# A three-layer block on one core: layer 2's attention takes its softmax sums and head outputs ahead of the convolution branch's steps, and the branch's roots go operation by operation

## The chip, the cores and the metric

One core of a Trainium2 chip runs the whole program in one launch. The time is the device time of one execution in microseconds (us). PE is the matmul engine (TensorE), DVE is VectorE, ACT is ScalarE, POOL is GpSimd, SP issues the DMAs. Every engine takes its own instructions strictly in the order in which the program lists them; engines wait for each other through semaphores.

## The reference

Three different layers run on 1024 tokens of 1024 features. The change is in the second, a hybrid layer. What matters of it:

```python
def hybrid_layer(h, cos, sin, chunk_id, ...):
    n = rms_norm(h, mix_norm_g)
    z = n @ w_in
    a, gate, c_q, c_kv, k_r = split(z)
    u = a * sigmoid(gate)                              # 512 features
    u = causal_depthwise_conv(u, conv_w, conv_b)       # 31 taps
    u = silu(layer_norm_2(u, conv_ln_g, conv_ln_b))    # over the 512 features
    q = rms_norm(c_q, q_norm_g) @ w_uq                 # 8 heads of 96
    kv = rms_norm(c_kv, kv_norm_g) @ w_ukv
    o = block_causal_attention(q, k, v, chunk_id)      # softmax(q k^T) v, chunks of 64
    mix = concatenate([rms_norm(u, conv_out_g), rms_norm(o, attn_out_g)])
    h = h + mix @ w_out
    ...                                                # then a feed-forward part
```

So the attention and the branch of `u` (convolution, layer norm, Silu, RMS norm) don't need each other before `mix`, and the kernel runs them side by side.

## The kernel before, in words

Data lie transposed: 128 features on the partitions, tokens along the free axis (1040 tokens here, in rows of 1044). `Mixer2` is layer 2's mixing part. Its attention has 8 heads. A head's keys go in three pieces of 4, 7 and 9 key tiles (`PIECES2`), so a head has 20 **slots** and the stage 160 (`CHUNKS2`); slot c is slot s of head h, with c = 20h + s. All three engines' programs (`pe` L1785, `act` L1960, `dve` L2185) are one loop over the slots, with the same things in the same slots:

- every slot: PE makes the scores of the chunk two slots on (`pe_chunk`), ACT takes their exponential (`act_exp`), and PE weighs the values with the chunk of this slot (`pe_weigh`).
- slots 0 to 5: the next head's keys (every second head) and queries on PE (`pe_next_head`, through one PSUM bank), copied by ACT and rotated by DVE (`act_products`, `dve_products`).
- slots 8 to 15: one block each of the next head's scores (`pe_score`), whose maxima DVE takes (`dve_max`). A score waits for the maximum two blocks back. In slots 15 and 18 PE turns the maxima into rows, which ACT copies.
- a piece ends in slots 3, 10 and 19. In the slot of the end ACT copies the weighed values and their sums (`act_head_copy`); the next piece's first `pe_weigh` waits for that copy. Two slots on PE turns the sums (`pe_column`) and DVE inverts them (`dve_inverse`); four slots on PE spreads the inverses (`pe_spread`) and DVE multiplies (`dve_head_out`). So DVE inverts in slots 5, 12 and 1 and writes head outputs in slots 7, 14 and 3.
- PE's chunks, rows, columns and spreads, and the branch's sums, take the same three PSUM banks in turn (`pe_ring` L1627): each waits until the one three before it has been copied or used.

Beside this runs the **branch**, written as a generator for each engine (`pe_branch` L1462, `act_branch` L1483, `dve_branch` L1515). `taps(c)` says how many of its steps slot c takes: `STEPS` of them are spread evenly over the first `LAST_STEP` = 140 slots, after 61 that run ahead of the attention. DVE's branch is 124 convolution taps, three adds, then per 128 features (4 of them) the centring and the adding of squares, the root of the variance (`root_newton` L409, four operations in a row), the scaling, again the adding of squares, a second root, and the last scaling. ACT's branch is the copies of the sums, the squares, the first guess of the root (Ln, then Exp), the four Silus in one step, four more squares and a second guess. PE's branch is three groups of three matmuls against ones. A `yield` ends a step, and bare `yield`s are the delays that hold the three engines' branches together:

```python
    def taps(self, c):
        done = [min(x, self.LAST_STEP) * self.STEPS // self.LAST_STEP for x in (c, c + 1)]
        return done[1] - done[0]
```

In the loops, `advance(branch, self.taps(c))` stands ahead of `pe_column` and `pe_spread` on PE, of `act_head_copy` on ACT, and of `dve_inverse` and `dve_head_out` on DVE.

Of the kernel before, what the change touches and what calls it, by code (L numbers as in the profile page):

```python
# [7 lines left out]
P = 128  # L8
# [8 lines left out]
LN_EPS, EPS = 1e-5, 1e-6  # L17
# [126 lines left out]
def advance(steps, n):  # L144

    for _ in range(n):
        if next(steps, None) is None:
            return
# [19 lines left out]
class Core:  # L168
# [240 lines left out]
    def root_newton(self, v, out, scratch, sums, n, eps, inc=None, sums_taken=None):  # L409
        v.tt(scratch, out, out, ALU.mult)  # L410
        v.settle()
        v.stt(scratch, sums, n * eps, scratch, ALU.add, ALU.mult, inc=sums_taken)
        v.settle()
        v.ts(scratch, scratch, -0.5 / n, 1.5, ALU.mult, ALU.add)
        v.settle()
        v.tt(out, out, scratch, ALU.mult, inc=inc)
        v.settle()

    def ones_of(self, view, pieces, banks):
# [961 lines left out]
class Mixer2:  # L1381
# [13 lines left out]
    SMALL = (0, 4, 8)  # L1395
    STEPS, LAST_STEP = 91, 140

# [64 lines left out]
    def pe_branch(self, t):  # L1462

        k = self.k
        for _ in range(CONV2 * 4 + 2):
            yield True
        for n, summed in enumerate((1, 8, 13)):
            t.wait_ge(self.u_step_v, summed)
            self.u_ring.append([])
            for t0, m in THREE:  # L1470
                r, bank = self.pe_ring(t)
                t.mm([(k.ps[:, bank, 0:m], k.ones[:, :], self.A[0][:, t0:t0 + m], True, True)], self.filled)
                self.u_ring[n].append(r)
            yield True
            for _ in range((5, 12, 0)[n]):
                yield True
# [6 lines left out]
    def act_branch(self, a):  # L1483
        k, A, M = self.k, self.A, self.M
# [8 lines left out]
        for n in range(2):  # L1493
# [5 lines left out]
            yield True  # L1499
            yield True  # L1500
            if n:
# [4 lines left out]
            for c in range(4):  # L1506
                a.act(M[c], M[c], ACT.Silu, scale=k.column("conv_ln_g_2", c), bias=k.column("conv_ln_b_2", c), inc=self.u_step_a)
            yield True
            a.settle()
# [5 lines left out]
    def dve_branch(self, v):  # L1515
# [23 lines left out]
        for n in range(2):  # L1539
# [3 lines left out]
            v.wait_ge(self.u_step_a, (5, 14)[n])  # L1543
            v.settle()
            k.root_newton(v, A[1], A[2], A[3], 4 * P, EPS, inc=self.u_step_v)
            yield True
            if n:
                break
            for c in range(4):
                v.tt(M[c], M[c], A[1], ALU.mult, inc=self.u_step_v if c == 3 else None)  # L1550
                yield True
            yield True
            for c in range(4):
# [231 lines left out]
    def pe(self, t):  # L1785
# [28 lines left out]
        for c in range(len(CHUNKS2)):  # L1814
# [9 lines left out]
            if h + 1 < H2 and s in self.ROW_AT:  # L1824
                for p in self.ROW_AT[s]:
                    self.pe_row(t, h + 1, p)
            advance(branch, self.taps(c))
            if self.ended(c - 2) is not None:
                self.pe_column(t, self.ended(c - 2))
            if self.ended(c - 4) is not None:  # L1830
                self.pe_spread(t, self.ended(c - 4))
            self.pe_weigh(t, c)
            k.label(("slot", c))
# [126 lines left out]
    def act(self, a):  # L1960
# [24 lines left out]
        for c in range(len(CHUNKS2)):  # L1985
# [6 lines left out]
            if h + 1 < H2 and s in self.ROW_AT:  # L1992
                for p in self.ROW_AT[s]:
                    self.act_row(a, h + 1, p)
            advance(branch, self.taps(c))
            if self.ended(c) is not None:
                self.act_head_copy(a, c)
            if c >= self.LAST_STEP + 4 and c % 4 == 0:
                self.act_u_row(a, (c - self.LAST_STEP) // 4 - 1)
# [185 lines left out]
    def dve(self, v):  # L2185
# [30 lines left out]
        for c in range(len(CHUNKS2)):  # L2216
            h, s = divmod(c, A_HEAD)
            self.dve_products(v, ("fill", c))
            if h + 1 < H2 and s in self.SCORE_AT:
                self.dve_max(v, item)  # L2220
                item += 1
            advance(branch, self.taps(c))
            if self.ended(c - 2) is not None:
                self.dve_inverse(v, self.ended(c - 2))
            if self.ended(c - 4) is not None:
                self.dve_head_out(v, self.ended(c - 4))
            if c >= self.LAST_STEP + 4 and c % 4 == 0:
                self.dve_u_row(v, (c - self.LAST_STEP) // 4 - 1)
# [1137 lines left out]
```

## Time and profile before

| | us |
|---|---|
| runs shown: median of 3 (lowest, highest) | 3708.06 (3707.95, 3716.88) |
| the profiled execution: its time | 3714.25 |
| its span (first to last instruction) | 3712.1 |
| PE busy in the span | 3475.0 |
| layer 2's attention, roughly | 1509 to 1830 of the span |

How to read it: PE is the engine that the whole kernel waits for in most places, so what PE loses in the attention is lost to the kernel. In the timeline rows, the number in brackets is the time for which the engine stood idle just before the instruction, and behind the arrow what ended that idle time. PEclk is the mean of the granted TensorE clock over a window, 1.00 being 2.4 GHz and 0.50 being 1.2 GHz. A busy time of PE includes what a lower clock adds. Lines are those of the kernel; helpers such as L96 (`tt`), L105 (`stt`), L124 (`act`), L129 (`copy`) and L136 (`mm`) carry most operations.

### The profile page before, as it was taken

To read this page: it belongs to the slowest core of one execution; us is meant where nothing else is said; L and a number is where in the kernel's file an instruction comes from. 1 tells how busy PE (TensorE), PEld (TensorE's weight loads), DVE (VectorE), ACT (ScalarE), POOL (GpSimd) and SP (SyncE) were. 2 spreads that over 40 slices of the span, in tenths; PEclk is the share of its full clock that TensorE was granted. 3 is DMA by queue.
4 is the path that set the end of the run, shared out by engine and by line. 5 is a ranking of instruction groups with operands and counts; after the bars stand their busy time and mean duration, and the time that the engine had idled before them with its cause. 6 is when DMAs were issued, how large, how long until landed. Compare 5 with 4: busy or idle time off the path is not lost.

```text
span 3712.1 us, 39245 instructions
## 1 busy us (share of the span) xinstructions
PE 3475.0 (94%) x16240; PEld 2806.7 (76%) x16240; DVE 1769.8 (48%) x1897; ACT 1119.0 (30%) x1492; POOL 1069.5 (29%) x1144
## 2 busy tenths in 40 slices
PE   9988999999999999898899999999998999999997
PEld 6655667888887688555588998998976777777776
DVE  4567562222223678686455544644664222443422
ACT  4333352111112522444531111111234222322332
POOL 3111343223323233000023433433432222211243
PEclk9999999999999999999899999999999999999999
DMA  3000211111111211000111111111121111100232
GB/s 121 23 24 28 103 62 63 51 47 46 49 48 58 75 63 40 12 6 6 58 40 40 46 46 51 41 49 49 46 91 35 68 57 40 35 24 28 85 122 93
DMA packets 56249, 192.21 MB, mean 52 GB/s; under 512 B 6900, under 2 KB 7284, under 8 KB 55560
## 3 DMA queue, kind: packets, MB, share of 16 engines
q1 hardware_dynamic: 56072, 189.71, 14.9%
q8 instruction: 128, 2.10, 0.2%
q14 instruction: 49, 0.40, 0.0%
HBM read 172.83 MB, written 16.86 MB: 51 GB/s over the span
## 4 chain that ended last, share of the span: by engine, by line
PE 78%; DVE 14%; ACT 5%; issue 2%; DMA 1%; POOL 0%; DVEq 0%; ACTq 0%; SPq 0%; POOLq 0%
PE psum L263 21%; PE psum L264 21%; PE psum L265 21%; PE psum L136 11%; DVE mix L105 3%; DVE work L96 3%; PE psum L305 2%; PE psum L307 1%; PE psum L306 1%; DVE res L96 1%; ACT L124 1%; DVE res L105 1%; DVE softmax_shift_columns L111 1%; DVE u_padded L96 1%; DVE work L114 1%
## 5 line engine op out<-in xcount | busy, mean ns | idle before, releaser
L96 POOL TENSOR_TENSOR w_lo<-w_raw,w_hi 128x256 fp32r<-128x256 f32 x1140 | 1069.3, 969 | 2607.7 <-ACT w_hi L129 2607.7
L263 PE MATMUL psum<-x_hi,w_hi 128*128 128x512 f32 (+2 forms) x3264 | 1229.6, 377 | 36.0 <-issue 6.8
L264 PE MATMUL psum<-x_lo,w_hi 128*128 128x512 f32 (+2 forms) x3264 | 1183.8, 363 | 0.0
L265 PE MATMUL psum<-x_hi,w_lo 128*128 128x512 f32 (+2 forms) x3264 | 1180.6, 362 | 0.0
L129 ACT CAST w_hi<-w_raw 128x1024 fp32r<-128x1024 f32 x285 | 298.2, 1048 | 1619.1 <-PE psum L265 1524.6
L263 PEld LDWEIGHTS psum<-x_hi,w_hi 128*128 128x128 f32 x3264 | 621.5, 190 | 141.5 <-issue 37.6
L264 PEld LDWEIGHTS psum<-x_lo,w_hi 128*128 128x128 f32 x3264 | 622.2, 191 | 91.0 <-issue 19.8
L265 PEld LDWEIGHTS psum<-x_hi,w_lo 128*128 128x128 f32 x3264 | 620.3, 190 | 78.7
L263 PE MATMUL psum<-h_hi,w_hi 128*128 128x512 f32 x848 | 338.3, 399 | 15.5 <-issue 9.0
L265 PE MATMUL psum<-h_hi,w_lo 128*128 128x512 f32 x848 | 336.0, 396 | 0.0
L264 PE MATMUL psum<-h_lo,w_hi 128*128 128x512 f32 x848 | 333.8, 394 | 0.0
L105 DVE SCALAR_TENSOR_TENSOR res<-res,psum 128x1024 f32<-128x1024 f32 (+1 forms) x88 | 90.3, 1027 | 253.6 <-PE psum L265 245.4
L263 PEld LDWEIGHTS psum<-h_hi,w_hi 128*128 128x128 f32 x848 | 160.0, 189 | 56.8 <-issue 13.2
L264 PEld LDWEIGHTS psum<-h_lo,w_hi 128*128 128x128 f32 x848 | 160.0, 189 | 40.0 <-issue 2.6
L265 PEld LDWEIGHTS psum<-h_hi,w_lo 128*128 128x128 f32 x848 | 159.9, 189 | 35.7
L136 PE MATMUL psum<-res 128*65 128x256 f32 (+5 forms) x480 | 171.5, 442 | 7.9 <-ACT res L129 4.2
L96 DVE TENSOR_TENSOR h_tmp<-h_tmp 128x1024 f32<-128x1024 f32 (+1 forms) x36 | 54.8, 1523 | 248.2 <-ACT h_tmp L124 248.2
L105 DVE SCALAR_TENSOR_TENSOR mix<-u_padded,vectors,mix 128x1044 f32<-128x1044 f32 x120 | 168.5, 1404 | 5.0 <-ACT work L129 0.8
L96 DVE TENSOR_TENSOR up<-psum,ffn_rms 128x1026 f32<-128x1026 f32 x44 | 54.0, 1227 | 204.7 <-PE psum L265 204.7
L105 DVE SCALAR_TENSOR_TENSOR up_conv<-up,vectors,up_conv 128x1024 f32<-128x1024 f32 x88 | 143.9, 1635 | 3.1
L305 PE MATMUL psum<-x_hi,w_hi 128*128 128x348 f32 (+2 forms) x304 | 122.7, 403 | 20.5 <-DVE x_lo L96 11.5
L96 DVE TENSOR_TENSOR res<-res,psum 128x1024 f32<-128x1024 f32 (+1 forms) x56 | 68.5, 1224 | 151.5 <-PE psum L265 148.5
(281 smaller groups left out, 3671.5 us busy)
## 6 DMA issues: line engine op xcount, KB each, us to landing
w_raw<-w_dram SPq DMA_DIRECT2D x285, 512.0 KB, 3.2
res<-spill SPq DMA_DIRECT2D x4, 1044.0 KB, 9.6
res<-x_dram SPq DMA_DIRECT2D x8, 512.0 KB, 7.7
res<-x_dram SPq DMA_DIRECT2D x4, 1024.0 KB, 8.2
spill<-res SPq DMA_DIRECT2D x1, 4096.0 KB, 13.9
spill_a<-mix SPq DMA_DIRECT2D x8, 512.0 KB, 2.6
res<-spill_a SPq DMA_DIRECT2D x8, 512.0 KB, 4.3
x_plain<-spill SPq DMA_DIRECT2D x4, 1024.0 KB, 10.9
```

The source lines that it names most:

```text
L96: self.mark(self.e.tensor_tensor(out, a, b, op), inc)
L105: self.mark(self.e.scalar_tensor_tensor(out, a, s, b, op0, op1), inc)
L111: self.mark(self.e.tensor_reduce(out, a, AX.X, op, negate=negate), inc)
L114: self.mark(self.e.reciprocal(out, a), inc)
L124: self.mark(self.e.activation(out, a, func, bias=bias, scale=scale), inc)
L129: self.mark(self.e.copy(out, a), inc)
L136: ins = self.e.matmul(out, lhsT, rhs, start=start, stop=stop, skip_group_check=True)
L263: t.e.matmul(out, whi, xhi, start=k == 0, stop=False, skip_group_check=True)
L264: t.e.matmul(out, whi, xlo, start=False, stop=False, skip_group_check=True)
L265: ins = t.e.matmul(out, wlo, xhi, start=False, stop=last_k, skip_group_check=True)
L305: t.e.matmul(out, whi, xhi, start=first, stop=False, skip_group_check=True)
L306: t.e.matmul(out, whi, xlo, start=False, stop=False, skip_group_check=True)
```

## The change

Four edits. In the slot loops of all three engines the branch's steps move behind the inverses and head outputs (DVE), the head copy (ACT), and the columns and spreads (PE). DVE's root becomes four steps instead of one (`root_steps`, new). The Silus go in two steps of two. The number of steps over the 140 slots goes from 91 to 98, and the delays on PE and ACT grow to match, so every step of the branch gets a new slot.

```diff
--- before.py
+++ after.py
@@ -415,6 +415,22 @@
         v.settle()
         v.tt(out, out, scratch, ALU.mult, inc=inc)
         v.settle()
+
+    def root_steps(self, v, out, scratch, sums, n, eps, inc=None):
+
+        v.settle()
+        v.tt(scratch, out, out, ALU.mult)
+        yield True
+        v.settle()
+        v.stt(scratch, sums, n * eps, scratch, ALU.add, ALU.mult)
+        yield True
+        v.settle()
+        v.ts(scratch, scratch, -0.5 / n, 1.5, ALU.mult, ALU.add)
+        yield True
+        v.settle()
+        v.tt(out, out, scratch, ALU.mult, inc=inc)
+        v.settle()
+        yield True
 
     def ones_of(self, view, pieces, banks):
         return [(self.ps[:, b, 0:m], self.ones[:, :], view[:, t0:t0 + m], True, True) for b, (t0, m) in zip(banks, pieces)]
@@ -1393,7 +1409,7 @@
     SCORE_AT = {8: 3, 9: 8, 10: 2, 11: 7, 12: 1, 13: 6, 14: 4, 15: 5}
     ROW_AT = {15: (0,), 18: (1, 2)}
     SMALL = (0, 4, 8)
-    STEPS, LAST_STEP = 91, 140
+    STEPS, LAST_STEP = 98, 140
 
     def __init__(self, core, ffn):
         self.k, self.ffn, s = core, ffn, core.s
@@ -1472,7 +1488,7 @@
                 t.mm([(k.ps[:, bank, 0:m], k.ones[:, :], self.A[0][:, t0:t0 + m], True, True)], self.filled)
                 self.u_ring[n].append(r)
             yield True
-            for _ in range((5, 12, 0)[n]):
+            for _ in range((5, 16, 3)[n]):
                 yield True
 
     def act_sums(self, a, n, out, scale):
@@ -1497,7 +1513,8 @@
             a.settle()
             k.root_guess(a, A[1], A[3], 4 * P, EPS, self.u_step_a)
             yield True
-            yield True
+            for _ in range(4):
+                yield True
             if n:
                 break
             for _ in range(4):
@@ -1505,7 +1522,8 @@
             a.wait_ge(self.u_step_v, 10)
             for c in range(4):
                 a.act(M[c], M[c], ACT.Silu, scale=k.column("conv_ln_g_2", c), bias=k.column("conv_ln_b_2", c), inc=self.u_step_a)
-            yield True
+                if c % 2:
+                    yield True
             a.settle()
             for c in range(4):
                 a.wait_ge(self.u_step_v, (10, 10, 11, 12)[c])
@@ -1541,14 +1559,13 @@
             yield True
             yield True
             v.wait_ge(self.u_step_a, (5, 14)[n])
-            v.settle()
-            k.root_newton(v, A[1], A[2], A[3], 4 * P, EPS, inc=self.u_step_v)
-            yield True
+            yield from k.root_steps(v, A[1], A[2], A[3], 4 * P, EPS, inc=self.u_step_v)
             if n:
                 break
             for c in range(4):
                 v.tt(M[c], M[c], A[1], ALU.mult, inc=self.u_step_v if c == 3 else None)
                 yield True
+            yield True
             yield True
             for c in range(4):
                 if c:
@@ -1824,11 +1841,11 @@
             if h + 1 < H2 and s in self.ROW_AT:
                 for p in self.ROW_AT[s]:
                     self.pe_row(t, h + 1, p)
-            advance(branch, self.taps(c))
             if self.ended(c - 2) is not None:
                 self.pe_column(t, self.ended(c - 2))
             if self.ended(c - 4) is not None:
                 self.pe_spread(t, self.ended(c - 4))
+            advance(branch, self.taps(c))
             self.pe_weigh(t, c)
             k.label(("slot", c))
         self.pe_column(t, 3 * H2 - 1)
@@ -1992,9 +2009,9 @@
             if h + 1 < H2 and s in self.ROW_AT:
                 for p in self.ROW_AT[s]:
                     self.act_row(a, h + 1, p)
-            advance(branch, self.taps(c))
             if self.ended(c) is not None:
                 self.act_head_copy(a, c)
+            advance(branch, self.taps(c))
             if c >= self.LAST_STEP + 4 and c % 4 == 0:
                 self.act_u_row(a, (c - self.LAST_STEP) // 4 - 1)
             k.cast(a, k.at["slot", c][0])
@@ -2219,11 +2236,11 @@
             if h + 1 < H2 and s in self.SCORE_AT:
                 self.dve_max(v, item)
                 item += 1
-            advance(branch, self.taps(c))
             if self.ended(c - 2) is not None:
                 self.dve_inverse(v, self.ended(c - 2))
             if self.ended(c - 4) is not None:
                 self.dve_head_out(v, self.ended(c - 4))
+            advance(branch, self.taps(c))
             if c >= self.LAST_STEP + 4 and c % 4 == 0:
                 self.dve_u_row(v, (c - self.LAST_STEP) // 4 - 1)
         self.dve_inverse(v, 3 * H2 - 1)
```

## Rows read from the trace of the kernel before

**Rows 1.** The page: busy time of each engine; the chain that ended last.

```profile
PE 3475.0 (94%) x16240; PEld 2806.7 (76%) x16240; DVE 1769.8 (48%) x1897; ACT 1119.0 (30%) x1492; POOL 1069.5 (29%) x1144
...
PE 78%; DVE 14%; ACT 5%; issue 2%; DMA 1%; POOL 0%; DVEq 0%; ACTq 0%; SPq 0%; POOLq 0%
```

**Rows 2.** Windows per head (3 to 6): us, busy of PE, PEld, DVE, ACT, POOL; PEclk.

```profile
1622.00:1660.00 38.00, 35.88 (x160) 23.16 (x159) 28.54 (x43) 16.84 (x46) 0.00 (x0) 0.91 0.01 1
1660.00:1697.00 37.00, 33.30 (x158) 20.03 (x156) 31.77 (x51) 14.36 (x44) 5.89 (x4) 1.00 0.04 15
1697.00:1748.00 51.00, 39.05 (x173) 24.16 (x172) 31.33 (x46) 27.85 (x61) 0.00 (x0) 0.93 0.00 0
1748.00:1800.00 52.00, 39.99 (x156) 23.00 (x157) 26.31 (x45) 30.47 (x56) 2.77 (x4) 0.83 0.03 11
```

**Rows 3.** Timeline of heads 4 and 5: start, length, engine, what, [idle before <-releaser].

```profile
1682.96 1.16 DVE L111 TENSOR_REDUCE softmax_shift_columns<-psum 128x1 fp32r<-128x960 f32 x1 [0.91 <-PE psum L136]
...
1695.39 0.70 PE L136 MATMUL psum<-work,x_plain 97*128 97x256 f32 x2 [1.56 <-DVE mix L96]
...
1702.78 0.43 PE L305 MATMUL psum<-x_hi,w_hi 128*128 128x348 f32 x1 [0.49 <-ACT x_hi L124]
...
1703.85 1.92 PE L136 MATMUL psum<-u_padded,ones 128*128 128x348 f32 x6
```

**Rows 4.** Groups of instructions from 1500 to 1835 us: busy, mean ns | idle before.

```profile
L105 DVE SCALAR_TENSOR_TENSOR mix<-u_padded,vectors,mix 128x1044 f32<-128x1044 f32 x61 | 82.0, 1345 | 2.9 <-ACT work L129 0.8
...
L96 DVE TENSOR_TENSOR u_padded<-u_padded 128x1044 f32<-128x1044 f32 x12 | 15.0, 1247 | 21.8 <-ACT u_padded L124 21.5
...
L124 ACT ACTIVATE u_padded<-mix 128x1044 f32<-128x1044 f32 x11 | 11.8, 1073 | 6.7 <-DVE mix L96 4.8 <-DVE u_padded L96 1.8
...
L124 ACT ACT_TABLE_LOAD x7 | 9.0, 1283 | 0.1
...
L124 ACT ACTIVATE mix<-mix,vectors 128x1044 f32<-128x1044 f32 x4 | 4.7, 1246 | 0.0
...
L124 ACT ACTIVATE u_padded<-u_padded,tiny 128x1044 f32<-128x1044 f32 x2 | 2.3, 1168 | 0.0
```

**Rows 5.** Timeline of heads 5 and 6: PE's waits, and one operation of a root.

```profile
1716.52 0.86 PE L136 MATMUL psum<-res 16*65 16x384 f32 x2 [1.08 <-ACT res L129]
...
1729.57 0.70 PE L136 MATMUL psum<-work,x_plain 97*128 97x256 f32 x2 [3.17 <-DVE mix L96]
...
1730.60 3.21 PE L136 MATMUL psum<-u_padded,ones 128*128 128x348 f32 x6
...
1742.08 0.70 PE L136 MATMUL psum<-work,x_plain 97*128 97x256 f32 x2 [1.77 <-ACT res L124]
...
1744.35 0.70 DVE L102 TENSOR_SCALAR u_padded<-u_padded 128x1044 f32<-128x1044 f32 x1
...
1747.89 1.22 PE L136 MATMUL psum<-work,x_plain 97*128 97x256 f32 x2 [4.17 <-DVE mix L96]
...
1756.95 0.43 PE L305 MATMUL psum<-x_hi,w_hi 128*128 128x348 f32 x1
...
1766.97 0.91 PE L136 MATMUL psum<-work,x_plain 97*128 97x384 f32 x2 [3.44 <-ACT res L124]
...
1770.11 1.54 PE L136 MATMUL psum<-res 16*65 16x384 f32 x2 [2.23 <-ACT res L129]
...
1783.09 0.70 PE L136 MATMUL psum<-work,x_plain 97*128 97x256 f32 x2 [0.41 <-DVE mix L96]
...
1793.80 0.70 PE L136 MATMUL psum<-work,x_plain 97*128 97x256 f32 x2 [1.77 <-ACT res L124]
...
1799.61 1.22 PE L136 MATMUL psum<-work,x_plain 97*128 97x256 f32 x2 [4.17 <-DVE mix L96]
```

**Rows 6.** Windows: slots 9 to 16 of head 1, and of head 6.

```profile
1573.00:1586.00 13.00, 12.10 (x51) 8.38 (x50) 12.29 (x25) 3.58 (x10) 0.00 (x0) 0.74 0.00 1
...
1782.00:1800.00 18.00, 11.65 (x57) 7.73 (x55) 13.38 (x25) 9.02 (x16) 0.00 (x0) 0.89 0.00 1
```

## The prediction

> **What bounds the kernel now.** Three views, in this order. The page: PE is busy for 94% of the span and holds 78% of the chain that ended last [rows 1], so a time won elsewhere counts only where PE waits for it. Windows over the attention, one per head, each from slot 16 of the head before to its own slot 15: head 3 takes 38 us and head 4 37 us, with the convolution's taps beside them, but heads 5 and 6, beside which the norms, roots and Silus run, take 51 and 52 us [rows 2]. That is 28 us more, of which PE's work is about 6 (the branch's matmuls against ones, one group of three 1.92) [rows 3]. The timeline says where the rest sits. In head 4 PE waits 1.56 us at slot 16 for the head output that DVE writes in slot 14 [rows 3]. In heads 5 and 6 it waits 1.08 us for a head copy that ACT makes after a square, 3.17 us for a head output behind DVE's additions, 1.77 us twice for an exponential behind Ln and Exp, 4.17 us twice for a head output behind the four operations of a root, and 3.44 and 2.23 us for ACT behind the Silus [rows 5]. The granted clock comes on top: 0.93 and 0.83 in these heads against 1.00 in head 4 [rows 2]. At two levels, 0.5 and 1, this is 7.1 and 17.7 us at 1.2 GHz, and the drops stand behind the waits: after the 2.23 us wait two matmuls take 1.54 us.
>
> **The new places.** With 98 steps over 140 slots, a slot takes 0.70 steps in place of 0.65, 14 per head in place of 13. Counting yields gives the slots. The taps end at slot 89 (was 96). First sums: 94 (was 101). Squares on ACT and centrings on DVE: 95, 97, 98, 99 (were 103, 104, 106, 107). Second sums 102 (110), Ln and Exp 104 (112), root on DVE 105, 107, 108, 109 (all in 113). Scaling 111, 112, 114, 115 (115 to 119). Silus 117 and 118 (all in 121). Second squares 119, 121, 122, 124 (123 to 127). Third sums 127 (130), Ln and Exp 128 (132), root 129, 131, 132, 134 (133). Last scalings end in slot 139 as before. What matters is the kind of slot: slots 0 to 5 of a head hold the next head's queries, about 3 us of PE each, slots 15 to 19 hold about 1 us of PE each. I work out PE's time part by part.
>
> **A. Heads 0 to 3: 0 us** (bounds -2 and +4). DVE is nearly full between slots 9 and 16: 12.3 of 13 us [rows 6]. From the start of the big maximum at 1682.96 to the head output are 12.4 us with four taps of 1.35 in them [rows 3, 4]. Afterwards three taps lie there (slots 9, 11, 12), since slot 13 has none and slot 14's stands behind the head output: -1.3. But the steps of slots 7 and 8 now lie ahead of the maximum with the head output of slot 7 in front: about +0.9. In heads 1 and 3 PE also runs at the lower level there (0.74) and is as late as DVE [rows 6], so these win nothing: 2 x -0.45. Against it, behind the head output DVE has five taps instead of four before the next rotation of queries, for which PE waits in two of the heads: about +1.
>
> **B. Slots 94 to 101: +8.3 us** (0 to +11). The three adds (3 x 1.25 [rows 4]) take the place of one tap in head 4, head output +0.65 later. The third group of ones needs the bank that this head output frees, so PE stands in slot 14 and not in 16, with about 2.6 us of work still ahead. Then the chain of squares: DVE centres (1.25), ACT squares (1.07), DVE adds (1.25), three times over: about 3.65 us a round [rows 4]. It used to lie beside queries; now it lies in slots 95 to 99, where PE needs about 5 us for all five. ACT takes its queue in order. Behind square 1 wait the exponential of slot 98 and the rows; behind square 2 the exponential of slot 99 and the head copy that slot 100 needs; behind square 3 the copy of the first keys, which frees the bank of the second. Laid out from the head output, with these lengths, square 1 ends at 7.7 us, square 2 at 11.3, square 3 at 14.8, and the second piece of keys starts at 17.0. Before, from the wait's end to that piece are 7.4 us [rows 3]. Of the 9.6 more, 1.92 are the first sums, which used to come right after it: +7.7, and with the 0.65 +8.3.
>
> **C. Head 5: -8.4 us** (-11.5 to -5). The four waits of 1.08, 3.17, 1.77 and 4.17 go [rows 5]: the head copy and head output stand in front of the step, the root is in four slices of at most 1.25, and Ln and Exp (two loads of 1.28, 1.17 and 1.07: 4.8 us of ACT [rows 4]) lie in a slot with queries. In their place: about 1.7 us in slot 106 or 107, where PE has 4.0 us of work against ACT's 5.75, and about 1.4 at slot 16, where DVE's chain is 10.8 us (12.4 less four taps, plus a slice and two scalings of 1.25). -10.2 + 3.1 = -7.1. The group of ones that took 3.21 us at 1.2 GHz takes 1.92: -1.3 [rows 3, 5].
>
> **D. The Silus: +2.0 us** (-5.7 to +9). The old waits of 3.44 and 2.23 go: -5.7 [rows 5]. But Silu and Exp alternate: slot 118's exponential lies between the two pairs, and each change of function has a load of 1.28 us in front [rows 4], four instead of two: +2.6 us of ACT. From slot 16's head output on: ACT ends its exponential at 1.7, loads, waits for the last scaling (3.9), does two Silus of 1.25 (6.4), loads, the exponential (8.2), rows, load, two Silus (12.6), load, exponential, head copy (14.8), square, copy of the queries (16.8). PE reaches the second piece of queries at 16.8 us; before it took 1756.95 - 1747.89 = 9.06 [rows 5]: +7.7.
>
> Of such loads the rule of the Trainium skill, ScalarE: Activation LUTs, section Rules for kernel authors, speaks against this split: do all functions of one table set before switching. The same page (What ACT_TABLE_LOAD costs) gives about 2.66 us a switch, load and drain; the row shows 1.28 and under 0.1 us of idle around it. By the page's figure the two extra switches would be an estimated 5.3 us instead of 2.6, and the sum of all parts about -0.2 us instead of -2.9.
>
> **E. Head 6: -3.9 us** (-6.4 to 0). Old waits: 1.77 + 4.17 and 0.41 behind a head output, 6.35 in all [rows 5]. Ln and Exp start four slots earlier, in slot 8; Exp ends some 5.2 us after slot 8's start, and behind it DVE has three slices (1.25, 1.25, 0.70) and 5.6 us of reductions and head output (12.4 less the taps and the first maximum), so slot 14's head output is done after 14.0 us, against 11.6 us of PE work [rows 5, 6]: about 2.4 remain.
>
> **F. The clock: -0.9 us** (-7 to +5). Old: 24.8 us at 1.2 GHz in heads 5 and 6, worth at most half. 1.3 of it is in C, 1.9 in D's 9.06; of the rest I take 6.9 as on PE's path. New knots of waits in B and D (each 5 to 9 us of waiting within 17) should bring drops as before, 3.4 to 6.8 us each, more after D: +6.0.
>
> **At nothing:** PE's columns and spreads, which moved only past matmuls of the branch; SP and POOL, which issue and do nothing for it (the branch has no DMA); the four slices of a root, which are the same four operations. If their cover goes, it is PE's wait for a spread, at most one operation of 1.25 us.
>
> **Sum:** 0 + 8.3 - 8.4 + 2.0 - 3.9 - 0.9 = **-2.9 us**. The profiled execution took 3714.25, so 3711.3 by its own time; it lies 6.2 us above the median of the runs shown, 3708.06. Carried to the median: **3705**. A measurement of this kernel tells about 0.3%, 11 us, from no change.
>
> **The rivals.**
> - **The waits go and none comes (24%).** If DVE and ACT run far enough ahead that B's chain ends under PE's next work, B is near 0 and D is two waits of 2 us. For it: chunks are made two slots ahead, and heads 3 and 4 cost 37 to 38 us. Against it: ACT's own idle time is small in slots with Silus. Of the 22 us of excess that isn't work, two thirds go: -15, so 3693.
> - **ACT's queue in short slots becomes the wait (18%), slower.** Place: slots 95 to 101 and 117 to 120. Its price is all three rounds of squares (3 x 3.65 = 11) and the full D at +4, with +4 of clock; C and E then give back only 5 and 2, as ACT starts them late. 11 + 4 + 4 - 5 - 2 = +12: 3720. It decides from the point at which PE passes slots 95 to 99 in 5 us and the copies of slots 99 and 100 stand behind squares 2 and 3. For it: the 1.08 us wait is this very thing in a longer slot.
> - **Nothing moves (15%).** Waits only change their names, as slots 9 to 16 are bound by DVE's reductions with or without a step among them: within 2 us, 3708.
> - **Forecast (43%):** gains and losses of 8 us cancel, 3705.
>
> The clock has a rival inside the forecast: if the knots in B and D bring no drop, F is -6.9 and the result is 3699. The Trainium skill, TensorE: Matmul & The Clock Gate, Terms, puts the penalty at the throttled time times (1 - K/N), here half. By that the old 24.8 us are worth 12.4 at most; rows agree on the factor, since matmuls there take twice as long, but PE was not always the bound.
>
> Range: 3690 (the first rival, a little past it) to 3720 (the second). Faster by over 0.3%: the first rival, 0.24. Slower: the second, 0.18. Same: 0.58.
>
> **What would show it.** Heads 0 to 4 unchanged within 1 us each. The four 1.77 and 4.17 waits gone, none over 2 us behind a head output in heads 5 and 6. PE waits for ACT at slots 98 to 101 of some 7 us in all, and at slots 118 to 121 of 8 to 10 us, with drops of the clock behind both. Nine table loads instead of seven. I am wrong in B if the second keys of head 5 start less than 12 us after the head output of head 4, in D if PE waits less than 5 us around the Silus, in A if the first four heads differ by over 4 us together.

## The result, and the profile after

The kernel before took 3712.12 us (median of 17 runs, 3707.06 to 3716.88), the changed one 3718.05 (17 runs, 3710.17 to 3726.10). The ratio is 1.0015, 95% interval 1.0009 to 1.0021: **5.6 us slower**, where 2.9 us faster was forecast. The 17 runs put the median of before 4 us above the three runs of the prediction. The profiled execution of the changed kernel took 3710.17, the shortest of its 17, so its span must not be compared as a whole; stage by stage it can.

The page has the same instructions as before, two more on ACT (the table loads), and 3.3 us more of PE [rows 1].

```profile
PE 3478.3 (94%) x16240; PEld 2810.0 (76%) x16240; DVE 1769.4 (48%) x1897; ACT 1121.9 (30%) x1494; POOL 1068.5 (29%) x1144
...
PE 78%; DVE 14%; ACT 5%; issue 2%; DMA 1%; POOL 0%; DVEq 0%; ACTq 0%; SPq 0%; POOLq 0%
```

Layer 2's attention, from its first row of maxima on PE to the first L263 matmul behind the last head, as one window. Columns: length; busy of PE, PEld, DVE, ACT, POOL; PEclk; DMA share; GB/s. Two profiles of the kernel before, the second taken later:

```profile
1509.03:1829.97 320.94, 280.30 (x1219) 168.89 (x1219) 216.85 (x334) 151.71 (x377) 19.82 (x16) 0.93 0.02 7
```

```profile
1512.62:1835.15 322.53, 281.85 (x1218) 169.71 (x1219) 216.82 (x334) 151.84 (x377) 19.83 (x16) 0.92 0.02 7
```

And three of the changed kernel:

```profile
1506.13:1833.54 327.41, 294.65 (x1219) 180.63 (x1219) 216.16 (x334) 154.51 (x379) 20.83 (x16) 0.89 0.02 7
```

```profile
1509.60:1837.42 327.82, 295.11 (x1218) 180.73 (x1218) 216.08 (x334) 154.50 (x379) 20.83 (x16) 0.89 0.02 7
```

```profile
1510.27:1837.66 327.39, 294.66 (x1219) 180.62 (x1219) 216.07 (x334) 154.50 (x379) 20.83 (x16) 0.89 0.02 7
```

The stage repeats within 1.6 us and is 5.8 us longer (327.5 against 321.7), which is the whole difference of the medians. Length less busy time is PE's idle time: 40.6 and 40.7 us before, 32.8, 32.7 and 32.7 after. So **the change took 7.9 us of waiting away from PE**. But the same 1219 matmuls are 13.7 us longer (294.8 against 281.1), and PEclk fell from 0.93 to 0.89. The granted clock has two levels here, 2.4 and 1.2 GHz, and the time at 1.2 GHz in the stage is 48 and 51 us before and 75 us in each of the three profiles after; half of the 25 us more is 12.6.

What costs is the part of that time in which PE has work. Before, PE was busy for 38.2 and 41.4 us of its time at 1.2 GHz, since waits lay in it; after, for 71.5, 72.2 and 71.6. Busy time less half of this, that is, PE's work at full clock, is 261.2 and 261.1 us before and 258.9 to 259.0 after. So the 5.8 us are 7.9 less of waiting, 2.3 less of work at full clock and 16.0 more for matmuls at 1.2 GHz. Both kernels have a stretch at 1.2 GHz near the end of head 6. In the kernel before it holds most of the 4.17 us wait that ends at 1799.61 [rows 5]; in the changed one it is full of work (8 matmuls, then 21):

```profile
1795.93:1802.75 6.82, 3.14 (x8) 1.96 (x8) 6.56 (x12) 0.76 (x4) 0.00 (x0) 0.50 0.00 0
```

```profile
1795.95:1802.77 6.82, 6.82 (x21) 5.30 (x22) 5.55 (x13) 1.15 (x3) 0.00 (x0) 0.50 0.00 0
```

By heads, each from the end of the head output of slot 14 (DVE) to that of the next head, for heads 5, 6 and 7; this is nearly the cut of [rows 2]:

```profile
1696.90:1751.81 54.91, 47.76 (x189) 29.51 (x188) 28.50 (x46) 29.33 (x66) 0.00 (x0) 0.84 0.00 0
1751.81:1804.28 52.47, 43.23 (x152) 26.72 (x153) 22.55 (x41) 32.58 (x57) 3.78 (x4) 0.77 0.03 10
1804.28:1828.51 24.23, 23.73 (x109) 12.61 (x107) 13.20 (x19) 13.04 (x37) 0.00 (x0) 1.00 0.00 1
```

Cut so, the first from the stage's start, heads 0 to 7 took 35.84, 39.62, 35.38, 39.61, 35.86, 52.49, 51.73, 25.38 us before and 35.30, 39.69, 37.81, 40.02, 37.95, 54.91, 52.47, 24.23 after. Head 7 took 26.9 us in the second profile of before, from a longer stretch at 1.2 GHz, and 24.2 to 24.3 in all three after, which have none there.

PE's waits in the timeline of heads 4 to 6 (start, length, what, idle before and who ended it):

```profile
1668.26 0.43 PE L305 MATMUL psum<-x_hi,w_hi 128*128 128x348 f32 x1 [1.62 <-DVE work L96]
...
1694.19 0.79 PE L136 MATMUL psum<-x_hi 96*128 96x512 f32 x1 [3.01 <-DVE softmax_shift_columns L96]
...
1695.42 3.69 PE L136 MATMUL psum<-u_padded,ones 128*128 128x348 f32 x6
...
1705.06 0.50 PE L136 MATMUL psum<-identity_rounded,softmax_shift_columns 128*1 128x128 f32 x5 [1.16 <-ACT res L124]
...
1715.16 0.66 PE L305 MATMUL psum<-x_hi,w_hi 128*128 128x348 f32 x1 [3.20 <-ACT x_hi L124]
...
1736.32 0.70 PE L136 MATMUL psum<-work,x_plain 97*128 97x256 f32 x2 [0.34 <-ACT res L124]
...
1751.86 0.70 PE L136 MATMUL psum<-work,x_plain 97*128 97x256 f32 x2 [0.29 <-DVE mix L96]
...
1759.87 1.65 PE L136 MATMUL psum<-work,x_plain 97*128 97x384 f32 x2 [4.41 <-ACT res L124]
...
1766.45 0.88 PE L136 MATMUL psum<-res 16*65 16x400 f32 x2 [1.07 <-ACT res L129]
...
1768.21 0.43 PE L305 MATMUL psum<-x_hi,w_hi 128*128 128x348 f32 x1 [0.46 <-ACT work L129]
...
1795.32 0.61 PE L136 MATMUL psum<-res 16*65 16x256 f32 x2 [2.02 <-ACT res L129]
```

What to see: the waits of 1.08, 3.17, 1.77, 4.17, 3.44 and 2.23 us [rows 5] are gone. New are 3.01 (a score in slot 14 of head 4), 3.20 (the second keys) and 4.41 (behind the Silus). And the first group of ones, 1.92 us before [rows 3], takes 3.69. ACT around the Silus:

```profile
1753.59 1.28 ACT L124 ACT_TABLE_LOAD   x1
1755.61 2.40 ACT L124 ACTIVATE mix<-mix,vectors 128x1044 f32<-128x1044 f32 x2 [0.73 <-DVE mix L96]
1758.03 1.28 ACT L124 ACT_TABLE_LOAD   x1
1759.32 0.49 ACT L124 ACTIVATE res<-psum 16x400 f32<-16x400 f32 x1
...
1760.59 1.28 ACT L124 ACT_TABLE_LOAD   x1
1761.89 2.40 ACT L124 ACTIVATE mix<-mix,vectors 128x1044 f32<-128x1044 f32 x2
1764.31 1.28 ACT L124 ACT_TABLE_LOAD   x1
1765.60 0.54 ACT L124 ACTIVATE res<-psum 64x64 f32<-64x64 f32 x2
```

It is the chain that the prediction laid out: load, two Silus, load, the exponential for which PE stands 4.41 us, and the same again.

### The profile page after: what moved, and what is told of

Read it like the earlier page. It is cut to its first block, busy times and chain, and to the rows that moved or that the text cites. A ratio compares the mean times of both kernels' runs of the same rounds, so it can differ in the third digit from the quotient of the medians.

```text
span 3708.1 us, 39248 instructions
## 1 busy us (share of the span) xinstructions
PE 3478.3 (94%) x16240; PEld 2810.0 (76%) x16240; DVE 1769.4 (48%) x1897; ACT 1121.9 (30%) x1494; POOL 1068.5 (29%) x1144
## 4 chain that ended last, share of the span: by engine, by line
PE 78%; DVE 14%; ACT 5%; issue 2%; DMA 1%; POOL 0%; DVEq 0%; ACTq 0%; SPq 0%; POOLq 0%
PE psum L263 21%; PE psum L265 20%; PE psum L264 20%; PE psum L136 11%; DVE mix L105 3%; DVE work L96 3%; PE psum L305 2%; PE psum L307 1%; PE psum L306 1%; DVE res L96 1%; ACT L124 1%; DVE res L105 1%; DVE softmax_shift_columns L111 1%; DVE work L114 1%; ACT res L124 1%
## 5 line engine op out<-in xcount | busy, mean ns | idle before, releaser
L263 PE MATMUL psum<-x_hi,w_hi 128*128 128x512 f32 (+2 forms) x3264 | 1227.6, 376 | 36.1 <-issue 6.8
L263 PEld LDWEIGHTS psum<-x_hi,w_hi 128*128 128x128 f32 x3264 | 620.5, 190 | 140.9 <-issue 37.2
L263 PE MATMUL psum<-h_hi,w_hi 128*128 128x512 f32 x848 | 337.7, 398 | 15.5 <-issue 9.0
L263 PEld LDWEIGHTS psum<-h_hi,w_hi 128*128 128x128 f32 x848 | 159.6, 188 | 56.7 <-issue 13.2
L96 DVE TENSOR_TENSOR h_tmp<-h_tmp 128x1024 f32<-128x1024 f32 (+1 forms) x36 | 55.1, 1531 | 249.3 <-ACT h_tmp L124 249.3
```

Source lines behind the costliest of these rows:

```text
L96: self.mark(self.e.tensor_tensor(out, a, b, op), inc)
L263: t.e.matmul(out, whi, xhi, start=k == 0, stop=False, skip_group_check=True)
```

## The experiments

Three theories stand in the expectations. **W**: waits and work alone count. **C**: what costs is the time that PE spends at 1.2 GHz. **O**: the new order costs by itself. "Stage" is the window above; "at 1.2 GHz" is its time there; "run at 1.2 GHz" is the mean over all timed runs (of before, 121) of 2 x (1 - granted clock) x time. Each ratio is against runs of before timed together with that kernel. A "long" slot is one of slots 0 to 5 of a head, which hold the next head's queries; a "knot" is a place where several waits follow each other; the "rhythm" is which slots get the branch's steps.

| kernel | median us (runs) | ratio to before [95%] | stage | PE busy | PE idle | at 1.2 GHz | run at 1.2 GHz |
|---|---|---|---|---|---|---|---|
| before | 3712.1 (17) | | 320.9, 322.5 | 280, 282 | 40.7 | 48, 51 | 227 |
| after | 3718.1 (17) | 1.0015 [1.0009, 1.0021] | 327.4 to 327.8 | 295 | 32.7 | 75 | 255 |
| order alone | 3719.8 (9) | 1.0023 [1.0013, 1.0032] | 326.6 | 288 | 38.1 | 62 | 244 |
| slices alone | 3716.0 (11) | 1.0010 [1.0001, 1.0019] | 324.9 | 284 | 41.2 | 45 | 221 |
| old places | 3712.8 (11) | 1.0007 [0.9997, 1.0017] | 320.8 | 288 | 32.7 | 55 | 239 |
| squares long | 3712.1 (11) | 1.0006 [0.9997, 1.0015] | 321.7 | 288 | 33.8 | 61 | 244 |
| Silus long | 3716.2 (11) | 1.0014 [1.0004, 1.0023] | 320.6 | 290 | 30.3 | 65 | 256 |
| both long | 3707.6 (11) | 0.9990 [0.9982, 0.9999] | 318.0 | 287 | 31.4 | 55 | 231 |

**Order alone.** The kernel before with only the moved calls, for example on ACT:

```diff
-            advance(branch, self.taps(c))
             if self.ended(c) is not None:
                 self.act_head_copy(a, c)
+            advance(branch, self.taps(c))
```

> The kernel before with only the order in the slots changed (sums, head copy and head output ahead of the branch's steps; 91 steps, root and Silus as before). Theory W (time in the stage follows PE's waits): the waits of 1.08 and 3.17 us in head 5 and 0.41 in head 6 go, the 4.17 and 1.77 us and the Silus' waits stay: 4 to 5 us of waits less, about 5 us faster than before. Theory C (what the change costs is PE's time at 1.2 GHz, which new places of waits bring): few waits move, so PE's time at 1.2 GHz from 1509 to 1834 us stays near the 49 us of before (73 in the change), and again 4 to 5 us faster. Theory O (the order itself delays DVE ahead of the big maximum, +0.9 us a head, and so costs in all heads): 0 to 4 us slower.

3719.8 us, so the new order in itself loses as much as the whole change. W and C both said 4 to 5 us faster and missed; O had the direction but neither the size (0 to 4) nor the places, since heads 0, 1, 3 and 4 are only 0.1 to 0.2 us longer and heads 2, 5 and 6 2.3, 1.1 and 0.9. Its idle time fell by 2.6 us; the 3.17 us wait became one of 3.63 and one of the two 4.17 us waits stayed. The time at 1.2 GHz did not stay near 49 us as C had it but rose to 62. In head 2 the 6.8 us at 1.2 GHz that in the kernel before end with head 1, in slots where PE waits for DVE, begin 6.8 us later, at the start of head 2, and fall on the chunks behind the head output, where PE has work.

**Slices alone.** The changed kernel with the three calls of `advance` back in their old places.

> The changed kernel with the attention's sums and values behind the convolution's steps again, as before the change: 98 slices, Silus two and two. If the order costs something of its own (theory O): the run is nearer to before, 3712, and head 2, which the order alone made 2.3 us longer, is 35.4 us again. If only the place of the 1.2 GHz stretches decides (theory C): the time goes with their sum in the stage by half of it, whatever that is: 320.9 - 8 + half of (sum - 48) us for the stage, within 2. If waits alone decide (theory W): the 1.77 and 3.17 us waits that the order removes come back, +3 to +5 over after: 3721 to 3723.

3716.0 us. The clock is as good as before (45 us), but idle time is 41.2 us: nothing of the 7.9 is won. By theory C I had taken the 8 us as given without the order, which makes a stage of 311; it was 324.9. W (3721 to 3723) missed too, and O only in part: head 2 came down to 36.35 us, not to 35.4, and the run is 4 us above before and 2 below after. The order and the slices take the waits away only together: -2.6 and +0.5 apart, -7.9 as one.

**Order and slices in the old places.** A table of slots in place of `STEPS`, 91 steps' rhythm, Silus together in slot 121:

```diff
-        done = [min(x, self.LAST_STEP) * self.STEPS // self.LAST_STEP for x in (c, c + 1)]
-        return done[1] - done[0]
+        return self.PLACES.count(c)
```

> The change with its order and its slices, but every step of the branch in the slot it had before (squares 103 to 107, root from 113 on, all Silus in 121, where queries are computed). Theory W: PE's waits of heads 5 and 6 are only those of the Silus (5.7 us) and of the two Ln and Exp (3.5), 12 us less than before: 10 to 14 us faster than before. Theory C: the same waits, and PE's time at 1.2 GHz falls below the 49 us of before: 12 to 16 faster. If the order and slices themselves cost (rival), it is within 3 us of before.

3712.8 us, stage 320.8. Its idle time is 32.7 us, that of the changed kernel to a tenth, yet the stage is 6.7 us shorter with 20 us less at 1.2 GHz. The waits that the change takes away go without its new rhythm; what the changed kernel loses against this one comes with the rhythm. But W and C, with 10 to 16 us of gain over before, both missed: the run is within 3 us of before, as the rival had it. The 7.9 us less of waiting are met by 7.0 us more of PE's busy time. That is again the clock: PE is busy for 53.1 us at 1.2 GHz against 38.2 and 41.4 before, though the stretches are only 5 us longer, and its work at full clock is 261.5 us against 261. Stretches that used to cover waits now cover work.

**One knot at a time into long slots.** The same table, with the squares in slots 100 to 103 and what follows them to 109; or with both Silu steps in slot 120 and the second squares in 121 to 124.

> The change with one block moved: the four squares and centrings go from slots 95 to 99 to slots 100 to 103, the second sums, Ln and Exp and root follow (104 to 109); all else as in the change. Theory W: the waits of 1.16, 0.62 and 3.20 us behind the squares go, about 4 us less, 1 to 3 us of new ones in slots 103 to 107: 2 to 4 us faster than the change, so 2 to 4 slower than before. Theory C: the 1.2 GHz stretches of 3.4 and 10.2 us that began at 1708 and 1715 go too, another 3 to 5 us: as fast as before or up to 3 us faster. Rival (queries' slots are no better): as slow as the change.

> The change with one block moved: both pairs of Silus go from slots 117 and 118 to slot 120, one behind the other, the squares follow in 121 to 124. Two table loads fewer (2.6 us of ACT). Theory W: PE's waits of 4.41, 1.07 and 0.46 us become one or two of together 4 to 6 us, as slot 120 has queries but the block is 7.5 us long: 0 to 2 us faster than the change. Theory C: the stretches of 1.2 GHz (6.8 and 3.4 us) stay, since the wait stays: the same 0 to 2. Rival (the two pairs' split is what costs): 5 or more us faster than the change.

3712.1 and 3716.2 us; stage 5.8 and 6.9 us shorter than after's, with the idle time changed by +1.1 and -2.4. Most of the gain is again PE's busy time, 6.9 and 4.5 us less. The squares came out as C had it, as fast as before. For the Silus the run fits W and C (0 to 2 us), the stage their rival (5 or more). Of their gain little reached the runs: their time at 1.2 GHz is 256 us, after's, though the stage has 10 less. What lies outside the stage must have had more; one profile doesn't show why.

> The changed kernel with the squares in slots 100 to 103, what follows them to slot 109, and both Silu steps in slot 120 with the squares behind them in 121 to 124: both knots that the change made are in long slots. If the two parts' gains add in the stage (after 327.4, squares alone 321.7, Silus alone 320.6): 315 us and 3706 for the run. If the 1.2 GHz stretches only move on (theory C): stage 318 to 326 us, with more than 60 us at 1.2 GHz in it, and the run 3712 to 3716.

3707.6 us, 10.4 us below after and faster than the kernel before by more than its interval. The stage fell by 9.5 us, its time at 1.2 GHz by 20 and its idle time by 1.4. The gains did not add to 315, as theory C had it, but the time at 1.2 GHz went lower than it allowed, and the run is shorter than its 3712 to 3716. By heads: the squares alone take 2.1 us off head 5 and 3.8 off head 6, the Silus alone 7.5 off head 6, both 2.1 and 7.6. So what the squares win in head 6 isn't won again beside the Silus.

```profile
1511.42:1829.46 318.04, 286.68 (x1218) 175.93 (x1219) 216.11 (x334) 151.88 (x377) 20.84 (x16) 0.91 0.02 7
```

**Work of no use in PE's idle time.** These kernels leave nothing out; they add matmuls whose product nobody reads, ahead of the slot's chunk:

```diff
+    def pe_idle_work(self, t, h, s):
+        if h < 6 and s in (10, 11, 12, 13, 14, 15, 16):
+            t.e.matmul(self.k.ps[:, 7, 0:512], self.ident_r[:, :], self.k.x_hi[:, 0, 0:512], start=True, stop=True, ...)
...
+            self.pe_idle_work(t, h, s)
             if c + 2 < len(CHUNKS2):
                 self.pe_chunk(t, c + 2)
```

| kernel | matmuls | median us (runs) | ratio to before [95%] | stage | PE idle | at 1.2 GHz |
|---|---|---|---|---|---|---|
| before, heads 0 to 5 | 42 | 3716.4 (11) | 1.0010 [1.0001, 1.0019] | 322.7 | 38.4 | 34 |
| before, heads 0 to 3 | 28 | 3715.8 (12) | 1.0008 [0.9999, 1.0017] | 322.0 | 39.2 | 41 |
| after, heads 0 to 5 | 42 | 3713.2 (11) | 1.0000 [0.9991, 1.0009] | 324.0 | 31.9 | 48 |
| after, heads 4 and 5 | 14 | 3719.8 (9) | 1.0027 [1.0017, 1.0036] | 327.0, 328.0 | 31.0, 30.4 | 75, 75 |
| after, heads 0 to 3 | 28 | 3710.7 (11) | 0.9992 [0.9983, 1.0001] | 323.9 | 30.2 | 58 |
| both long, heads 0 to 5 | 42 | 3705.5 (11) | 0.9986 [0.9978, 0.9995] | 317.9 | 30.1 | 34 |
| both long, heads 0 to 3 | 28 | 3705.9 (12) | 0.9982 [0.9974, 0.9990] | 317.6 | 32.0 | 37 |

> The kernel before with one more 128x512 matmul in each of slots 10 to 16 of heads 0 to 5 (42 in all, each about 0.27 us at 1.9 GHz), ahead of the slot's chunk: TensorE idles there for VectorE in heads 0 to 3. Its product is read by nobody. Theory C (what costs is the time that TensorE spends at 1.2 GHz, which follows its idle stretches): the time at 1.2 GHz in the stage falls from 47.9 us to 30 or less and the time by up to 9 us: 3702 to 3708 against 3712 median of before. Theory W (only waits and work count; the clock is chance that an edit of this kind does not steer): no difference in heads 0 to 3 and, in heads 4 and 5, whose slots have no idle time, 14 x 0.27 = +4 us: 3716. If the clock is unmoved and the slots are full: up to +11 us.

> The kernel after with the same 42 extra matmuls. Theory C: the time at 1.2 GHz in the stage falls from 74.6 us to 45 or less, and the run gets 5 to 12 us shorter than after: 3706 to 3712, the loss of the change gone. Theory W: +4 us or more over after's 3718: 3722. The difference between the changed and the unchanged kernel, both filled, is by theory C about -8 (the waits that the change takes away) and by theory W the same as without the fillers, +6.

(The 0.27 us are an estimate that no row shows by itself; the clock's levels here are 1.2 and 2.4 GHz.)

The same addition did opposite things. Before got 4 us longer: W's number, but not by W's way, since heads 4 and 5 are 0.4 us longer together and the stage is as long as in the second profile of before. After got 5 us shorter, 1 us above C's range. Filled, the changed kernel is 3 us faster than the unchanged one, where C had said 8 faster and W 6 slower. In the kernel before, the 6.8 us at 1.2 GHz at the ends of heads 1 and 3 vanished and these heads stayed at 39.6 us: those stretches lay where PE waited for DVE and had cost nothing. In the changed kernel head 5 fell from 54.9 to 51.7 us.

> The changed kernel with the extra matmuls in heads 4 and 5 alone (14 instead of 42). Where in heads 0 to 3 the clock drops in slots that wait for VectorE anyway, it should cost nothing there: then these 14 give the whole gain of the 42, run 3713 and head 5 at 51.7 us against 54.9 of after. If the drops of heads 0 to 3 cost too, or carry over into head 5, the gain is smaller: 3715 to 3718, head 5 at 53 us or more.

> The changed kernel with the extra matmuls in heads 0 to 3 alone (28). They took the stretches at 26 and 105 us away when all 42 were there, and the heads stayed as long as they were. If early stretches cost nothing and carry nothing over: 3718, as after, with head 5 at 54.9 us. If they carry over (a later stretch goes or moves because an earlier one went): head 5 or what is behind the stage gets shorter, run 3712 to 3715.

The first missed both its forecasts (3713, and 3715 to 3718): 3719.8. The second is the telling one. None of the 28 matmuls is in head 5, heads 0 to 4 are as long as in the changed kernel, and head 5 is 3.3 us shorter. Head 5 of the kernel with them (compare the first of the three rows by heads above):

```profile
1699.75:1751.37 51.62, 44.26 (x189) 27.31 (x188) 28.48 (x46) 29.14 (x66) 0.00 (x0) 0.89 0.00 0
```

The same 189 matmuls, 3.5 us less of PE. Where the time at 1.2 GHz went is seen one head earlier. Head 4 in the changed kernel, then with the 28 matmuls:

```profile
1658.95:1696.90 37.95, 32.02 (x140) 19.43 (x141) 32.90 (x49) 12.81 (x38) 5.89 (x4) 0.96 0.05 14
```

```profile
1661.82:1699.75 37.93, 34.70 (x140) 21.18 (x141) 32.89 (x48) 12.81 (x38) 5.89 (x4) 0.88 0.05 14
```

Head 4 has 6.1 us more at 1.2 GHz (9.5 against 3.4) and is as long as before, as PE waits less there (3.2 us against 5.9); head 5 has 6.1 us less (11.0 against 17.1). The two heads together have what they had, 20.5 us: the stretches moved from work onto a wait.

The run is 7 us shorter than after's, more than its stage gave (3.7); the rest is outside. What the matmuls did where they are, the same 7 us of head 0 (about its slots 10 to 14), in the changed kernel and then with them:

```profile
1532.13:1539.13 7.00, 7.00 (x24) 4.94 (x22) 6.64 (x13) 0.77 (x2) 0.00 (x0) 0.57 0.00 0
```

```profile
1535.16:1542.16 7.00, 6.94 (x34) 4.87 (x35) 6.64 (x13) 1.15 (x3) 0.00 (x0) 1.00 0.00 0
```

The clock stayed at 2.4 GHz instead of falling to 1.2, and 34 matmuls took the time of 24. DVE, for which PE waits here, had 13 operations in either. The 14 matmuls of heads 4 and 5 alone won nothing: the first profile had a shorter head 5 (51.5 us) but longer heads 3 and 4, from stretches at 1.2 GHz that came ahead of any added matmul. Was that the program or the draw?

> The kernel with 14 extra matmuls, profiled again. If the stretches are set by the program: at 122 and 163 us again, heads 3 and 4 at 41.6 and 39.3 us. If they are a draw of that execution: heads 3 and 4 as in the changed kernel, 40.0 and 37.9, head 5 at 51.5, and the stage 324.

> The changed kernel, profiled a third time. If set by the program: the same stretches as in the two profiles before it, stage 327 to 328 us, about 75 us at 1.2 GHz. If a draw: another stage length, between 313 and 325.

> The kernel before, profiled again. If the stretches at 1.2 GHz follow the program, they fall at the same places of the stage (69, 144, 223, 236, 260 and 288 us behind its start) within a few us and sum to 45 to 51 us; if they are chance, they fall elsewhere and the sum is anywhere from 35 to 75.

> The kernel after, profiled again. If the stretches at 1.2 GHz follow the program: at 28, 69, 86, 107, 148, 189, 202, 209, 253, 264, 274 and 291 us behind the stage's start and 70 to 80 us in sum, the stage 327 us. If they are chance: other places, a sum of 45 to 80, and a stage of 313 to 330 us that goes with half the sum; the waits of TensorE (3.01, 3.20, 4.41 us) are the same in either case.

All three profiles of the changed kernel have their stretches within 1 us of the same places, and the two of before theirs (the last 3.4 us longer in the second). The kernel with 14 had them in the changed kernel's places the second time, with a head 5 of 55.1 us. So in this stage the program sets them nearly always, and the first profile was an exception; what makes one is open. Outside the stage they do vary: the whole of the three profiles of the changed kernel holds 233, 264 and 257 us at 1.2 GHz, 158 to 188 of it outside the stage, and their times are 3710.2, 3717.5 and 3717.7 us.

> The kernel before with the extra matmuls in heads 0 to 3 alone. Its stretches at 68 and 143 us lie in slots that wait for VectorE, and with all 42 matmuls they were gone and nothing shorter. If the matmuls undo a loss that the change brought: 3712 to 3714, no gain, and the changed kernel with them (3710.7) is 1 to 4 us faster than this one. If they are a gain for any kernel of this kind: 3705 to 3708.

> The changed kernel with both knots in long slots and the extra matmuls in heads 0 to 3 alone. If their effects add (both long: 10 us off after; these matmuls: 7 off after): 3700 to 3703. If the stretches only find other places: 3705 to 3708, as with both long alone or with all 42.

Before: 3715.8, no gain, and 5 us slower than the changed kernel with the same 28 matmuls. So they undo a loss that the change brought. With both knots in long slots they give 3705.9, as all 42 do (3705.5): the stretches only find other places, and the effects don't add. For the 42 theory C had said 20 us less at 1.2 GHz, a stage 3 us shorter and 3703 to 3709: the first and last came, but the stage stayed (317.9 against 318.0), as PE's busy time went up by 1.1 us. The two kernels with both knots in long slots and added matmuls are the fastest of the study, 0.14 and 0.18% below the kernel before, 12 us below the changed one.

## Why the prediction was wrong

**The step that failed is F, the clock.** Forecast: old drops worth 6.9 us given back, "new knots" charged 6.0, so -0.9. Measured: 25 us more at 1.2 GHz in the stage and PE's busy time 13.7 us longer; the clock cost about +12 us (see the sum). Three things in the step were wrong. Its sizes: it took drops of 3.4 to 6.8 us for a knot, but around B's waits three stretches have 20.4 us at 1.2 GHz, and head 6, behind the Silus, went from 17.6 to 23.9. Its places: all three profiles have new stretches also at 27, 85 and 105 us behind the stage's start, in heads 0 and 2, for which the prediction had put zero. Where they lie, only the one at 85 us costs (3.4 us long, on keys and queries), since heads 0 and 2 are as long without the other two, which the 28 matmuls took away. In head 0 no wait is new; in head 2 the one for the queries' rotation grew from 0.47 to 1.63 us, as forecast in A, and the 1.57 us one for the head output went. And it treated the clock as the waits' shadow, which should lighten when waits go. In the whole-stage rows, less waiting and more time at 1.2 GHz stand together, and a stretch that held a wait before holds work after.

The factor was right. PE's busy time in the stage, less half of its busy time at 1.2 GHz, is 261 us in both profiles of before, 259 in after's three, and 259 to 262 in the others without added matmuls: within 3.2 us, where the busy times themselves spread over 15. The Trainium skill, TensorE: Matmul & The Clock Gate, Terms, prices a throttled time at (1 - K/N) of itself, here half; these rows agree for busy time. For the length they agree only where PE is the bound: in heads 1 and 3 of before such stretches cost nothing.

**A, heads 0 to 3: 0 forecast (-2 to +4), +2.4 measured,** all in head 2, whose drop falls on keys and queries and whose wait for the rotation is 1.2 us longer. DVE's side was right: heads 1 and 3 are +0.1 and +0.4. The sign "heads 0 to 4 unchanged within 1 us each" failed in heads 2 and 4.

**B, squares: +8.3 forecast.** The sequence held. PE stands in slot 14, the group of ones follows, and the second keys start 18.3 us after head 4's output (17.0 forecast, 7.4 before). That is 8.9 more without the first sums, against 7.7; head 4's own output is 2.1 later instead of 0.65, with the ones at 3.69 us where 1.92 was counted. Together +11.0, which is the price that the slower rival had put on the squares; 1.8 of it is the ones at 1.2 GHz. The waits for ACT there are 1.16, 0.62 and 3.20 us, 5.0 in all against the 7 named as a sign.

**C, head 5: -8.4 forecast.** The four waits went. From the second keys to head 5's output it is 36.7 us against 45.1 less the 1.9 of the sums: -6.5, with head 5 at a clock of 0.84 against 0.94.

**D, Silus: +2.0 forecast.** The second queries start 16.4 us after head 5's output (16.8 forecast). PE's waits around the Silus are 4.41, 1.07 and 0.46 us, 5.9 in all: above the 5 under which D would have been wrong, below the 8 to 10 named. Four loads of 1.28 us stand where laid out. The Trainium skill, ScalarE: Activation LUTs, What ACT_TABLE_LOAD costs, adds a drain to a total of about 2.66 us. Here each exponential starts 0.01 us after its load's end (1758.03 + 1.28, 1759.32), so the trace charges the load alone, and the prediction's choice of the row was right. The page's rule against the split is not shown by itself: the run with both Silu steps in one slot has two loads less and a stage 6.9 us shorter, but also another slot.

**E, head 6: -3.9 forecast.** The 1.77 and 4.17 us waits left one of 2.02. D and E together: -1.9 forecast, +0.7 measured, the head's clock being 0.77 against 0.83. Head 7, which no part of the prediction has, is 1.9 us shorter.

**Sum.** A to E were forecast at -2.0. The stage's length less half its time at 1.2 GHz went from 296.9 to 290.1, -6.8, and the clock took +12.6: +5.8. Half of all time at 1.2 GHz is too much where PE waits or is covered, so this is cross-checked by PE's busy time: in heads 4 to 7 half of what it is busy at 1.2 GHz is 10.3 us more, and with 1.7 for the stretch at 85 us the clock cost +12.0 and the rest -6.2. Either way the rest did better than forecast, and the clock ate it. How the 6 us divide among B to E is less sure, as the forecast counted 1.3 and 1.9 us of the old drops in C and D. The slower rival came near the time (3720), but by another way: it named ACT's queue in short slots, whose place and price for the squares were seen (3.20, 4.41), while it gave C and E only -7 together and the clock +4. PE's waiting fell altogether, so it isn't the cause.

What stays open is what sets off a given stretch: PE was busy 9.2, 8.1 and 9.6 of the 10 us ahead of the drops at 27, 85 and 105 us, and before, with 9.9, 9.5 and 9.6 at the same places, no drop came. Nor is shown why runs of before got 3 to 4 us longer with matmuls that the stage hid.

## What to carry to other kernels

Where PE is busy nine tenths of the time and its clock still drops, read a stage as three numbers: busy, idle, and busy at 1.2 GHz. A stretch at 1.2 GHz that lay on a wait was free here; with the wait gone it was paid. A change that only moves instructions can win the idle time and lose more than that in the clock; forecast the waits, and give the clock a range of its own as wide as half of what the stage already spends at 1.2 GHz. And before a better schedule is thrown away, try it with its knots a few slots on: the same idea was 6 us slower and 4 us faster here.

## What the runs showed of the hardware that was not expected

In this stage the stretches at 1.2 GHz belong to the program: in three profiles of one kernel they came within 1 us of the same thirteen places, 75 us in sum each time, while the rest of the run held 158, 188 and 182. One profile of another kernel had other places than its second, so it is no law. They also reach ahead: 28 matmuls of no use in heads 0 to 3, hidden in PE's waits, moved 6 us at 1.2 GHz from head 5 onto a wait in head 4 and made head 5 3.3 us and the run 7 us shorter; the same 28 in the kernel before gave nothing. And matmuls at 1.2 GHz cost just double: PE's work at full clock comes out within 3.2 us in eight kernels whose busy times spread over 15.
